# A gated unit on rounded operands, an output projection group by group, and a branch split one group sooner

## The reference, cut to what matters

```python
# end of the S5 branch: gelu, then the gated unit (w_glu is 512 x 512)
y = jax.nn.gelu(y)
y = y * jax.nn.sigmoid(y @ w_glu)
# merge of the branches
merged = (jax.nn.sigmoid(za) * (y_a @ w_branch_a)
          + jax.nn.sigmoid(zb) * (y_b @ w_branch_b)
          + jax.nn.sigmoid(zc) * (y_c @ w_branch_c))
# end of the cross-attention (w_co is 1024 x 1024)
o = jnp.einsum('bhtm,bmhd->bthd', p, mv).reshape(B, T, D_MODEL)
x = x + o @ w_co
```

## Time and profile before

| what | value |
|---|---|
| device time, median of 3 runs | 2406.34 us (2405.97 to 2407.32) |
| device time of the profiled execution | 2406.9 us |
| its span, first to last instruction | 2405.1 us |
| TensorE busy (matmuls) | 2270.8 us, 94% of the span |
| VectorE, ScalarE, GpSimd busy | 48%, 25%, 12% of the span |
| mean granted TensorE clock | 0.975 of full speed |

### The profile page before, as it was taken

How to read it: one execution, slowest core, us unless ns; L and a number is a source line. 1 busy time by engine, 2 the same in 40 slices (tenths; PEclk the granted TensorE clock), 3 DMA queues, 4 the chain that set the end, 5 groups by cost and what they waited for, 6 DMA issues and landing times.

```text
span 2405.1 us, 34367 instructions
## 1 busy us (share of the span) xinstructions
PE 2270.8 (94%) x14712; PEld 2182.0 (91%) x14712; DVE 1142.9 (48%) x1264; ACT 596.2 (25%) x739; POOL 282.6 (12%) x436
## 2 busy tenths in 40 slices
PE   5799989999999999999999977899999999999995
PEld 5699979888989999999999966899999999999995
DVE  4716433334444344225644222436666556556665
ACT  4422223222322222223322122322111111111112
POOL 6989700000000000001000000000000000000000
PEclk9899999999989999999999999999999999999997
DMA  6311123112332222224321133011111111111111
GB/s 230 105 44 54 53 87 110 63 57 80 115 117 71 80 82 89 106 106 176 132 79 70 53 158 140 24 57 45 44 53 45 44 45 46 52 44 45 47 45 71
DMA packets 45221, 190.36 MB, mean 79 GB/s; under 512 B 5136, under 2 KB 5200, under 8 KB 41488
## 3 DMA queue, kind: packets, MB, share of 16 engines
q1 hardware_dynamic: 32112, 117.13, 14.1%
q0 software_dynamic: 11104, 54.41, 6.0%
q10 hardware_dynamic: 1872, 16.83, 1.8%
HBM read 152.59 MB, written 35.93 MB: 78 GB/s over the span
## 4 chain that ended last, share of the span: by engine, by line
PE 87%; DVE 4%; issue 4%; ACT 3%; DMA 1%; POOL 0%; ACTq 0%; DVEq 0%; POOLq 0%
PE ps L256 24%; PE ps L257 23%; PE ps L259 23%; PE ps L2059 1%; PE ps L1715 1%; PE ps L1006 1%; PE ps L371 1%; PE ps L372 1%; PE ps L374 1%; ACT PA L2126 1%; DVE WL L250 1%; DVE GT L399 1%; ACT WH L245 1%; ACT TMP L390 0%; PE ps L1691 0%
## 5 line engine op out<-in xcount | busy, mean ns | idle before, releaser
L256 PE MATMUL ps<-XH,WH 128*128 128x344 f32 x1656 | 535.7, 326 | 8.3 <-DVE WL L250 5.8
L257 PE MATMUL ps<-XL,WH 128*128 128x344 f32 x1512 | 481.1, 321 | 0.0
L256 PE MATMUL ps<-XN,WH 128*128 128x344 f32 x1248 | 399.0, 322 | 3.9 <-issue 3.7
L257 PE MATMUL ps<-XN,WH 128*128 128x344 f32 x1248 | 396.9, 321 | 0.0
L250 DVE TENSOR_TENSOR WL<-WRAW,WH 128x1024 fp32r<-128x1024 f32 x175 | 222.2, 1270 | 308.3 <-ACT WH L245 307.6
L259 PE MATMUL ps<-XH,WL 128*128 128x344 f32 x1656 | 352.9, 321 | 0.0
L256 PEld LDWEIGHTS ps<-XH,WH 128*128 128x128 f32 x1656 | 314.1, 190 | 19.5 <-issue 14.4
L245 ACT ACTIVATE WH<-WRAW 128x1024 fp32r<-128x1024 f32 x175 | 184.4, 1054 | 537.1 <-PE ps L259 522.4
L257 PEld LDWEIGHTS ps<-XL,WH 128*128 128x128 f32 x1512 | 286.5, 189 | 0.2
L259 PEld LDWEIGHTS ps<-XH,WL 128*128 128x128 f32 x1656 | 279.1, 189 | 0.0
L259 PE MATMUL ps<-XN,WL 128*128 128x344 f32 x1248 | 264.0, 319 | 0.0
(11 more groups left out here) (514 smaller groups left out, 3172.6 us busy)
## 6 DMA issues: line engine op xcount, KB each, us to landing
WRAW<-in_wslabs SPq DMA_DIRECT2D x175, 512.0 KB, 3.5
scratch_spill<-STAGE SPq DMA_DIRECT2D x40, 516.0 KB, 2.6
ZS<-scratch_spill POOLq DMA_DIRECT2D x24, 516.0 KB, 5.4
XIN<-in_xT POOLq DMA_DIRECT2D x1, 4128.0 KB, 18.5
XR<-in_xT ACTq DMA_DIRECT2D x2, 2064.0 KB, 8.5
out_y<-XR SPq DMA_DIRECT2D x8, 516.0 KB, 3.0
CACHES<-in_ck ACTq DMA_DIRECT2D x4, 1024.0 KB, 14.2
CACHES<-in_cv ACTq DMA_DIRECT2D x4, 1024.0 KB, 11.9
```

What stands on the lines that cost most here:

```text
L256: pe.matmul(out[t], WH[:, slot, w, :], xh(k, t), start=(k == 0), stop=False)
L257: pe.matmul(out[t], WH[:, slot, w, :], xl(k, t), start=False, stop=False)
```

## The change

There are three edits.

**1. The gated unit becomes a split product.** Its weights join the slab stream as two slabs (`SL_GLU`, two output groups each), between those of the mLSTM keys and values, so that slabs and fill order behind them move by two. `WPL`, its four loads and the product on L1006 go. ScalarE applies gelu to quarter q-1 of `SUT` in quarter q, behind the copy of `US`, and to the last quarter at the end. The last add of a quarter (L913) moves ahead of VectorE's slab split; in the last quarter ScalarE's evacuation of fill group 7 moves behind the first rounding. New are four roundings (`SUH`), four subtractions (`SUL`) and 144 matmuls in place of 48. The groups m = 0 and 1 run side by side, k-step by k-step; 2 and 3 follow in turn. The gated result goes back into `SUT`, and `YC` goes. `SUH` and `SUL` lie where `MKV` does, so its load moves behind the last group; `MQ` lies where `SUT` does, so its load now waits until the store of `yc` has landed. ScalarE's wait for that store ahead of the value projection goes.

**2. The branch split** takes parts 0 and 1 behind the first `SL_GR` group, part 2 behind the second, part 3 behind the third, none behind the fourth.

**3. The cross-attention's output projection** starts with `pe_start`: group 0 over all 8 k-steps, each as its part comes, then group 1. It is the code that `pe_out`, the projection of the merge, had already; that one stays as it is.

```diff
+        def pe_start(pe, n0, g0, ks, xl):
+            for s in range(2):
+                n, g = n0 + s, g0 + s
+                pe.wait_ge(w_lo, n + 1)
+                pe.wait_ge(acc_free[g % 2], g // 2)
+                for k in range(KT):
+                    if s == 0:
+                        pe.wait_ge(xl_ready, KT * ks + k + 1)
+                    last = split_step(pe, banks(g % 2), n % 2, xh_cols, xl, k, k, KT)
+                last.then_inc(acc_ready, 1)
...
-            for m in range(2):
-                pool.dma_start(WPL[:, m], I["wplain"][m]).then_inc(wp_loaded[m], 16)
...
-            pool.dma_start(MKT, I["spill"][4:8].rearrange("h p n -> p h n")).then_inc(mk_in, 16)
...
+                if q:
+                    act.wait_ge(s5_done, q)
+                    nc.scalar.activation(SUT[:, q - 1, :], SUT[:, q - 1, :], ACT.Gelu_apprx_tanh).then_inc(glu_in, 1)
...
         def pe_glu(pe):
             pe.wait_ge(fl_free, 8)
-            pe.wait_ge(s5_done, 4)
-            pe.wait_ge(glu_in, 4)
-            for m in range(4):
-                plain_product(pe, 16 * (m // 2 + 1), GR_GLU + m, m % 2, (GR_GLU + m) % 2,
-                              lambda k, t: SUT[:, k, t * TG:(t + 1) * TG])
+            def step(m, k):
+                return split_step(pe, banks((GR_GLU + m) % 2), (SL_GLU + m // 2) % 2,
+                                  lambda k, t: SUH[:, k, t * TG:(t + 1) * TG],
+                                  lambda k, t: SUL[:, k, t * TG:(t + 1) * TG], 4 * (m % 2) + k, k, 4)
+            pe.wait_ge(w_lo, SL_GLU + 1)
+            for k in range(4):
+                pe.wait_ge(glu_lo, k + 1)
+                for m in range(2):
+                    last = step(m, k)
+                    if k == 3:
+                        last.then_inc(acc_ready, 1)
+            pe.wait_ge(w_lo, SL_GLU + 2)
+            for m in range(2, 4):
+                pe.wait_ge(acc_free[(GR_GLU + m) % 2], (GR_GLU + m) // 2)
+                for k in range(4):
+                    last = step(m, k)
+                last.then_inc(acc_ready, 1)
...
         def pool_glu(pool):
-            for m in range(2, 4):
-                pool.wait_ge(acc_ready, GR_GLU + m - 1)
-                pool.dma_start(WPL[:, m % 2], I["wplain"][m]).then_inc(wp_loaded[m % 2], 16)
+            pool.wait_ge(acc_ready, GR_GLU + 4)
+            pool.dma_start(MKT, I["spill"][4:8].rearrange("h p n -> p h n")).then_inc(mk_in, 16)
         def pool_store_yc(pool):
             pool.wait_ge(glu_out, 4)
-            pool.dma_start(I["yc"], YC[:]).then_inc(yc_stored, 16)
+            pool.dma_start(I["yc"], SUT).then_inc(yc_stored, 16)
+            pool.wait_ge(yc_stored, 16)
             pool.dma_start(MQT, I["spill"][0:4].rearrange("h p n -> p h n")).then_inc(mq_in, 16)
...
-                act_part_hi(act, 0, (m,))
+                act_part_hi(act, 0, ((0, 1), (2,), (3,), ())[m])
...
-                dve_part_lo(dve, 0, (m,))
+                dve_part_lo(dve, 0, ((0, 1), (2,), (3,), ())[m])
...
-            pe_first(pe, SL_CO, G_CO, 4, xlo_cols)
+            pe_start(pe, SL_CO, G_CO, 4, xlo_cols)
```

More of the change, by code:

```diff
@@ L52 @@
 SL_SU = 17
-SL_MQ, SL_MV = 21, 29
-SL_GQ, SL_GKV = 33, 35
-SL_MO = 41
-SL_Z = 45
-SL_GR = 69
-SL_GATE = 73
+SL_MQ, SL_GLU, SL_MV = 21, 29, 31
+SL_GQ, SL_GKV = 35, 37
+SL_MO = 43
+SL_Z = 47
+SL_GR = 71
+SL_GATE = 75
 SL_OUT = SL_GATE + 12
@@ L914, in dve_s5 @@
                                                op0=M, op1=AD).then_inc(s5_done, 1)
+                if q < 3:
+                    dve_fill(dve, f"s{q}g")
         def pe_s5(pe):
@@ L992, in pe_s5 @@
                 pe.transpose(ps[:, 7, 0:8], USS2[:, :], IDENT[0:8, 0:8]).then_inc(s5_pe, 1)
-        YC = area("YC", [128, 4, N], 8256)
+        SUH, SUL = area("SUH", [128, 4, N], 4 * N, F32R), area("SUL", [128, 4, N], 8 * N, F32R)
         glu_in, glu_sig, glu_out, yc_stored = sem("glu_in"), sem("glu_sig"), sem("glu_out"), sem("yc_stored")
-        def plain_product(pe, n, g, slot, gslot, rhs):
-            pe.wait_ge(wp_loaded[slot], n)
-            pe.wait_ge(acc_free[gslot], g // 2)
-            for k in range(4):
-                for t in range(NTG):
-                    last = pe.matmul(banks(gslot)[t], WPL[:, slot, k, :], rhs(k, t), start=(k == 0), stop=(k == 3))
-            last.then_inc(acc_ready, 1)
+        glu_hi, glu_lo = sem("glu_hi"), sem("glu_lo")
@@ L1017, in act_glu, with hi @@
         def act_glu(act):
+            def hi(q):
+                nc.scalar.activation(SUH[:, q, :], SUT[:, q, :], ACT.Copy).then_inc(glu_hi, 1)
             act.wait_ge(s5_done, 4)
-            for q in range(4):
-                nc.scalar.activation(SUT[:, q, :], SUT[:, q, :], ACT.Gelu_apprx_tanh).then_inc(glu_in, 1)
+            act.wait_ge(glu_in, 3)
+            hi(0)
+            act_fill(act, "s3g")
+            hi(1)
+            hi(2)
+            nc.scalar.activation(SUT[:, 3, :], SUT[:, 3, :], ACT.Gelu_apprx_tanh).then_inc(glu_in, 1)
@@ L1021, in act_glu @@
+            act.wait_ge(glu_in, 4)
+            hi(3)
             for m in range(4):
@@ L1025, in act_glu, with dve_glu_lo @@
                 nc.scalar.activation(t3(TMP[:, m % 2, :]), acc((GR_GLU + m) % 2), ACT.Sigmoid).then_inc(glu_sig, 1)
+                if m % 2:
+                    act_hi(act, None, (SL_GLU + m // 2) % 2, 16 * ((SL_GLU + m // 2) // 2 + 2), None)
+        def dve_glu_lo(dve):
+            for q in range(4):
+                dve.wait_ge(glu_hi, q + 1)
+                nc.vector.tensor_tensor(SUL[:, q, :], SUT[:, q, :], SUH[:, q, :].bitcast(F32),
+                                        ALU.subtract).then_inc(glu_lo, 1)
+                if q == 0:
+                    dve_fill(dve, "s3g")
         def dve_glu(dve):
+            dve.wait_ge(glu_in, 4)
             for m in range(4):
@@ L1954, in pe_out @@
         def pe_out(pe):
-            for s in range(2):
-                n, g = SL_OUT + s, G_OUT + s
-                pe.wait_ge(w_lo, n + 1)
-                pe.wait_ge(acc_free[g % 2], g // 2)
-                for k in range(KT):
-                    if s == 0:
-                        pe.wait_ge(xl_ready, KT * 2 + k + 1)
-                    last = split_step(pe, banks(g % 2), n % 2, xh_cols, xl_cols, k, k, KT)
-                last.then_inc(acc_ready, 1)
+            pe_start(pe, SL_OUT, G_OUT, 2, xl_cols)
             pe_project(pe, SL_OUT + 2, G_OUT + 2, KT - 2)
@@ L2504, in half @@
         return w.reshape(4, 128, -1, 128).transpose(2, 1, 0, 3)
+    glu = half(f["s5_w_glu"][0])
+    glu = np.stack([np.concatenate([glu[m], glu[m + 1]], 1) for m in (0, 2)])
     gate = []
```

15 lines of the change are left out of this document (7 added, 8 removed).

## The result

The changed kernel took 2381.69 us (median; 2376.0 to 2383.45), beside 2406.15 us for the kernel before in the same measurement: 0.9891 of the time, 95% interval 0.9876 to 0.9907. Applied to the 2406.34 us of before, that is 2380.1 us. A second measurement gave 2376.37 us and 0.9873 [0.9857, 0.9888].

The account below looks back on a forecast made before the run. TensorE was taken as the bound, through its own work, standstills and the low-clock stretches behind them. The gains 9.6 + 7.2 + 5.3 = 22.1 us gave 2384.3, stated as 2384.5 us, with a range of 2381 to 2391.5.

Parts of the forecast that it names:

- Part 1: Gated unit: earlier start and less work bring the value projection from 377.08 to 367.4; gain 9.6 us, bounds 7.5 and 10.8.
- one low stretch behind it: Gated unit's product: after the 2.9 us standstill TensorE runs at clock 0.50 for 3.4 us, costing 1.5 us.
- A rule against the trace: Gated unit: the skill's 0.146 us per matmul would make 144 matmuls take 21.0 us; the trace's 0.157 us was kept.
- The hand-offs between ScalarE and VectorE: Gated unit: parts reach TensorE with 0.4 us of waiting; a further us of hand-offs was in the lower bound.
- the clock holds: Gated unit: no low stretch after the 2.9 us standstill; gain 10.8 in place of 9.6 us, 2383.3; chance 0.15.
- Part 2: Branch split ahead of the merge: wait of 5.1 us and low stretch of 2.1 us go; gain 7.2, bounds 5.1 and 7.2.
- Part 3: Cross-attention's output projection, third group: wait of 3.79 us and low stretch of 1.5 go; gain 5.3, bounds 3.8 and 5.3.
- a new wait: At the merge or the gated unit's hand-offs, a wait replaces one removed: up to 2391.7, or 2388.5; chance 0.12.
- serial transfers: Behind the gated unit, three 2 MB transfers in a row hold mLSTM: 10 us slower, 2416; chance of slower 0.03.
- a part that does not do what it says: Output projection's third group waits for something else, so 5.3 us stay: 2389.6; chance 0.05.
- the last term of the range: Anywhere in the kernel: 2 us below 2383 for a low stretch elsewhere that may not come again, giving 2381.
- the lower ends of the parts: The three parts' lower bounds, 7.5 + 5.1 + 3.8 = 16.4 us, giving 2390.

Follow-up runs that it names:

- after with one small matmul: The changed kernel with one small matmul more at the start, moving TensorE's code behind it by 4 instructions; 2379.12 us, 0.9901.
- the filler: The changed kernel with 17 thrown-away matmuls of 344 columns ahead of the gated unit's waits, so TensorE does not stand still there; 2382.16 us, 0.9896.
- the part alone: The kernel before with only the output projection's edit, `pe_first` replaced by `pe_start`; 2400.76 us, 0.9973.

## Why the prediction was right in its parts and short in its sum

- **Bound**: right. What the three edits gained came from TensorE's standstills, its low stretches and its own work, as the sum had it.
- **Part 1**: 9.6 forecast (the times given, 377.08 and 367.4, make 9.7), 9.7 and 9.6 us in two profiles up to the mLSTM rows, 9.4 up to the value projection. Standstill 2.9 against 2.84 us, one low stretch behind it as said. At full clock throughout (after with one small matmul, below) the 144 matmuls took 22.96 us, waits between them included, for 22.6 in the sum. The 21.0 us of the paragraph "A rule against the trace" did not come. The value projection started at 366.65 for 367.4 (S5 ended 1.0 us sooner). The hand-offs between ScalarE and VectorE held, `MQ` landed at 392.8 for 396, and TensorE waited 1.12 us at the rows.
- **The rival "the clock holds"** came true once in the nine profiles with the split product and its standstill of 2.84 us, in after with one small matmul: the same standstill, then full clock, and a product of 22.96 us instead of 24.41, 1.45 us for the forecast 1.5:

```profile
343.01 0.40 PE L254 MATMUL ps<-SUH,WH 128*128 128x344 f32 x1 [2.84 <-DVE SUL L1062]
...
365.97 0.32 PE L254 MATMUL ps<-XH,WH 128*128 128x344 f32 x1
```

  The value projection starts 26.03 us behind the transpose both here and with the filler, so the filler's full clock is no proof that filling the standstill kept it. The Trainium skill, "TensorE: Matmul & The Clock Gate", section "What's actually happening", lets the point of the change differ; this pair agrees.
- **Part 2**: 7.2 forecast, 7.4 us. **Part 3**: 5.3 forecast, 5.8 us in this profile and 5.5 with the part alone. The rivals of a new wait, of serial transfers and of a part that does not do what it says fell.
- **The step that failed** is the last term of the range: "with 2 us below for a low stretch elsewhere that may not come again". It stood for everything that a shift in time or in code does to untouched stages. It measured 3.7 us in the mLSTM and GLA stages and 3.4 us in the feed-forward block, 7 us where 2 were allowed and 0 entered the sum. With the 1.0 us ahead of the gated unit and 0.8 us more from the parts that makes, to rounding, the profile's 30.9 us for the 22.1 of the sum. The first could have been asked of the trace of before: three low stretches with 27.3 us between 426 and 686, of which I priced none. The second stood there as four waits at `issue` in the feed-forward loop, 3.7 us, and I did not ask whether moved code would keep them. Their sign could not have been told from that trace; their size could, and the range should have reached some 5 us further on each side. Its upper end was loose as well: the lower ends of the parts give 2390, not 2391.5.
- **Not explained**: the -1.0 us ahead of the gated unit; why a low stretch fell into S5's third quarter in two profiled kernels and more of them into the cross-attention in one, some 4 us each; and which of all this lies behind the single runs, 2402.4 to 2409.7 us for before in one measurement. Open too are the 5.3 us between the two medians of the changed kernel, 2381.69 and 2376.37 us: both its profiles are of runs near the lower one. No kernel here is faster than the changed one clear of the noise; its eight runs lie between 2374.9 and 2383.5 us.

## What to carry to other kernels

Price each edit by the stretch that it touches, then ask the trace what the untouched rest has that hangs on timing or on code position (low stretches behind small standstills, `issue` waits at a loop's head), and put the sum of both into the range, on both sides. When an edit's stage comes out as priced and the whole does not, compare the profiled run with its median, then cut both traces at the same instructions before looking for a cause in the edit. A difference under 0.2% between two versions may be only such a shift: test it by moving the start or the code and nothing else.
